# The order of a mixer's steps: from a written table to a rule of turns

## The reference

```python
h = rmsnorm(x, g_mix[l]) * (1.0 + sc1) + sh1
proj = h @ w_in[l]
q, k, v, u, c_gate, b_gate = jnp.split(proj, [A, 2 * A, 3 * A, 3 * A + C, 3 * A + 2 * C], axis=-1)
...
attn = moba_attention(heads(q), heads(k), heads(v), slopes)
attn = attn.transpose(0, 2, 1, 3).reshape(B, S, A)
conv = b_gate * causal_dwconv(c_gate * u, conv_w[l], conv_b[l])
mixed = jnp.concatenate([rmsnorm(attn, g_attn_out[l]), rmsnorm(conv, g_conv_out[l])], axis=-1)
x = x + gt1 * (mixed @ w_out[l])
```

## Time and profile before

| | |
|---|---|
| median of 3 runs | 1716.35 us |
| the profiled execution's own time | 1716.84 us |
| its span, first to last instruction | 1715.0 us |
| TensorE busy | 1676.2 us (98%) |
| VectorE, ScalarE, GpSimd busy | 1293.7 us, 929.3 us, 407.1 us |
| mean granted TensorE clock | 0.99 of full speed |
| this mixer's stretch | 1382 to 1514 us |

### The profile page before, as it was taken

One profiled execution on the slowest core, in us unless ns is written; L12 is line 12 of the kernel. 1 busy time (PEld: TensorE's weight loads), 2 busy tenths in 40 slices (PEclk: granted clock), 3 DMA queues, 4 the chain that ended last, 5 costly groups with the idle time before them and its releaser, 6 DMA issues.

```text
span 1715.0 us, 32702 instructions
## 1 busy us (share of the span) xinstructions
PE 1676.2 (98%) x13812; PEld 1523.4 (89%) x13812; DVE 1293.7 (75%) x2141; ACT 929.3 (54%) x1666; POOL 407.1 (24%) x316
## 2 busy tenths in 40 slices
PE   7999999999999999999999999999999999979997
PEld 6888998889898888888898888999888899979987
DVE  5887767866858877788776786686888776889974
ACT  5775435433546764577444543355675456466652
POOL 2763000000214661167200000021575100211110
PEclk9999999999999999999999999999999999989999
DMA  7675532211156655566562321125665553345442
GB/s 263 218 298 185 210 122 99 100 51 52 69 185 259 253 199 196 211 251 233 186 216 97 111 87 51 52 81 191 234 257 191 190 186 133 114 148 186 168 154 107
DMA packets 45057, 282.67 MB, mean 165 GB/s; under 512 B 6128, under 2 KB 6768, under 8 KB 18544
## 3 DMA queue, kind: packets, MB, share of 16 engines
q1 hardware_dynamic: 44912, 280.60, 45.3%
HBM read 279.53 MB, written 1.05 MB: 164 GB/s over the span
## 4 chain that ended last, share of the span: by engine, by line
PE 90%; DVE 6%; ACT 2%; issue 1%; DMA 1%; POOL 0%; SPq 0%; DVEq 0%; ACTq 0%
PE banks L457 28%; PE banks L458 14%; PE banks L992 11%; PE banks L449 7%; PE banks L450 7%; PE banks L451 7%; PE banks L1599 4%; DVE WL L420 2%; ACT WH L415 1%; PE banks L1868 1%; PE banks L496 1%; PE banks L1878 1%; DMA ring<-wst 1%; PE banks L664 0%; DVE XN L2502 0%
## 5 line engine op out<-in xcount | busy, mean ns | idle before, releaser
L420 DVE TENSOR_TENSOR WL<-ring,WH 128x2048 fp32r<-128x2048 f32 (+1 forms) x219 | 459.8, 2111 | 110.5 <-ACT WH L415 110.4
L457 PE MATMUL banks<-XNP,WH 128*128 128x512 f32 x1408 | 499.3, 399 | 10.8 <-DVE XNP L542 8.6
L415 ACT ACTIVATE WH<-ring 128x2048 fp32r<-128x2048 f32 (+1 forms) x223 | 380.8, 1716 | 55.8 <-PE banks L451 46.2
L458 PE MATMUL banks<-XNP,WL 128*128 128x256 f32 x1408 | 393.4, 279 | 0.0
L457 PEld LDWEIGHTS banks<-XNP,WH 128*128 128x128 f32 x1408 | 266.4, 189 | 73.0 <-DVE XNP L542 9.5
L890 POOL TENSOR_TENSOR HP<-G,HP 128x256 fp32r<-128x256 f32 x110 | 210.1, 1911 | 310.3 <-ACT HP L702 310.3
L457 PE MATMUL banks<-HP,WH 128*128 128x512 f32 x770 | 267.5, 392 | 0.8 <-POOL HP L890 0.7
L458 PEld LDWEIGHTS banks<-XNP,WL 128*128 128x128 f32 x1408 | 267.1, 190 | 0.0
L458 PE MATMUL banks<-HP,WL 128*128 128x256 f32 x770 | 215.2, 280 | 0.0
L992 PE MATMUL banks<-XN,ring 128*128 128x256 f32 x832 | 192.5, 381 | 0.0
L457 PEld LDWEIGHTS banks<-HP,WH 128*128 128x128 f32 x770 | 144.6, 188 | 33.3 <-POOL HP L890 1.4
(11 more groups left out here) (496 smaller groups left out, 3255.3 us busy)
## 6 DMA issues: line engine op xcount, KB each, us to landing
ring<-wst SPq DMA_DIRECT2D x205, 1024.0 KB, 4.9
ring<-wst SPq DMA_DIRECT2D x80, 704.0 KB, 4.0
LP<-lp SPq DMA_DIRECT2D x1, 1872.0 KB, 7.4
LP<-lp SPq DMA_DIRECT2D x4, 448.0 KB, 5.6
ring<-wst SPq DMA_DIRECT2D x2, 512.0 KB, 5.5
X<-xin SPq DMA_DIRECT2D x2, 512.0 KB, 6.3
out<-X SPq DMA_DIRECT2D x4, 256.0 KB, 2.2
C<-cst SPq DMA_DIRECT2D x1, 193.0 KB, 5.0
```

The lines of the kernel that those rows point to most:

```text
L415: e.do.activation(WH[:, slot[q], 0:n], ring[:, i % NSLOT, 0:n], ACT.Copy).then_inc(*w_act.up("high", q))
L420: e.do.tensor_tensor(WL[:, slot[q], 0:n], ring[:, i % NSLOT, 0:n], WH[:, slot[q], 0:n].bitcast(F32), ALU.subtract).then_inc(*w_dve.up("low ...
L457: e.do.matmul(b[:, :], WH[:, s, cols], x.rearrange("p s t -> p (s t)"), start=first, stop=False)
L458: return e.do.matmul(b[:, 0:T], WL[:, s, cols], x[:, 0, :], start=False, stop=last)
```

## The change

The table is replaced by a function that builds the list. `in_turns` goes round a fixed cycle of names; each time it comes to a name whose strand has steps left and whose need is met (counts of steps done by other strands), it appends that name. `second_order_of` gives the cycle and the needs.

```diff
+def in_turns(steps, turns, needs, allowed=None):
+    done, out = dict.fromkeys(steps, 0), []
+    while any(done[s] < steps[s] for s in steps):
+        before = len(out)
+        for turn in turns:
+            s = turn.split()[0]
+            if s != turn and not allowed(turn, done):
+                continue
+            if done[s] < steps[s] and needs(s, done[s], done):
+                out.append(s)
+                done[s] += 1
...
+    turns = ["proj", "conv", "att0", "att1", "proj", "att2", "att3", "norm0", "first", "norm1"]
...
+        if s == "conv":
+            return done["proj"] >= min(2 * in2_at(5, k) + 4, steps["proj"])
+        if s in attends:
+            j = attends.index(s)
+            return done["proj"] >= {0: 2 * in2_at(1, j) + 4, 4: 2 * in2_at(2, j) + 6}.get(k, 0)
+        if s == "norm1" and k == 0:
+            return done["conv"] == steps["conv"] and done["first"] >= 6
+        if s == "norm1" and k == 2:
+            return done["first"] == steps["first"]
+        if s == "norm0" and k == 0:
+            return all(done[n] == steps[n] for n in attends)
+        if s == "first":
+            return done["proj"] == steps["proj"] and done["norm0"] == steps["norm0"]
...
-SECOND_TURNS = """
-proj*10 att1 att0 proj*3 att1 proj*3 att0 proj*2 att1 proj*2 att0 att1 att3 proj*6 att0 att3*2 att2 att1 att0
...
-            orders[l] = turns(MIXER_TURNS) if l < DEPTH else turns(SECOND_TURNS)
+            orders[l] = turns(MIXER_TURNS) if l < DEPTH else second_order_of(steps)
```

More of the change, by code:

```diff
@@ L188, in wait_ge, with second_order_of, needs @@
             self.do.wait_ge(sem, n)
+def in_turns(steps, turns, needs, allowed=None):
[9 more added lines that the diff above has]
+                done[s] += 1
+        assert len(out) > before, done
+    return out
+def second_order_of(steps):
+    attends = [f"att{j}" for j in range(4)]
+    turns = ["proj", "conv", "att0", "att1", "proj", "att2", "att3", "norm0", "first", "norm1"]
+    def needs(s, k, done):
+        if s == "conv":
[11 more added lines that the diff above has]
+            return done["proj"] == steps["proj"] and done["norm0"] == steps["norm0"]
+        return True
+    return in_turns(steps, turns, needs)
 MIXER_TURNS = """
@@ L204 @@
 fin ssd fin*2 ahead*4 fin ahead*2
-"""
-SECOND_TURNS = """
-proj*10 att1 att0 proj*3 att1 proj*3 att0 proj*2 att1 proj*2 att0 att1 att3 proj*6 att0 att3*2 att2 att1 att0
-att1 att0 att1 proj att2 proj att3 proj att1 proj att0 proj*2 att0*2 proj*2 att2*2 att0 att3 att2 att3 att2
-proj att3 att1 proj att2 proj*3 att2 att3 proj att3 proj*2 att2 att3 conv*2 att1 att2 proj norm0 proj norm0
-proj*2 norm0 proj*2 first conv first*3 conv first*2 norm1 first*2 norm1*2
 """
```

## The result

The changed kernel has a median of 1725.14 us over 5 timed runs (1723.57 to 1726.16), the kernel before 1716.35 us (1714.70 to 1716.84) beside it. The ratio is 1.0052, with a 95% interval of 1.0040 to 1.0063: slower. The forecast was 1721.2 us with a range of 1718.0 to 1724.4. The sign and the places of the three waits were right; the size was too small by 3.9 us, and the range ended 0.7 us too low.

What follows compares the result with a forecast made beforehand. TensorE was taken to bound the projection stretch. Waits of 0.93 + 1.66 + 1.54 = 4.13 us plus 0.72 for scattering gave +4.85, so 1721.7 us for the profiled execution and 1721.2 for the median, range 1718.0 to 1724.4.

Steps and rivals of the forecast that it cites:

- the three waits: New TensorE waits at tile 6 and at pairs 2 and 3's first products with v: 4.13 us together.
- TensorE sets the pace of the stretch: From second to last projection tile TensorE is busy 80.96 of 81.20 us, so each new wait counts in full.
- tile 6: Projection tile needing tile 4's bias, its evacuation queued behind scores on VectorE: wait 1.17 us instead of 0.24, net +0.93.
- the products with v: Pairs 2 and 3's first products, close behind ScalarE's copy of v: waits of 1.66 and 1.54 us.
- Scattering: Eight more returns of TensorE to the projection at 0.09 us each: +0.72 us, bounds 0 and 0.8.
- The end of the list: Behind the last projection tile, conv 3 and norm1 1 earlier: cost 0, hidden by VectorE's 2.19 us idle.
- Rival A: The waits come and TensorE's clock falls to half in the stretch too: 1722.9 to 1724.6 us; chance 15%.
- Rival B: Waits in the stretch shrink to little as VectorE and ScalarE have free time: +0.5 to +3 us; chance 17%.
- Rival C: Faster: shifted clock fall at norm1 frees up to 2.2 us of VectorE's wait for the norm's row, 1713.9 us; chance 6%.

Runs made afterwards that it cites:

- e1: The changed kernel again with no edit, for a second profile: 1724.11 us, ratio 1.0047 to the kernel before.
- e3: Changed kernel with pairs 0 and 1's second-head scores one projection step earlier and pair 3's first product with v one later: 1720.42 us, ratio 1.0019.
- e4: Changed kernel with the edits of e3, and the first scores of pairs 0 and 1 together again as before: 1720.87 us, ratio 1.0023.
- e7: Kernel before with the transposes of pair 1's second head moved into the group of pair 0's, one break fewer: 1716.28 us.
- e8: Kernel before with only the changed list's end (conv 3 two steps earlier, norm1 1 ahead of first 7): 1715.48 us.
- e12: The changed kernel's order with the same added filler matmuls as e11: 1722.16 us, ratio 1.0022.
- e11: Kernel before with the filler matmuls of e9 and e10, plus two ahead of the mixer's first tile: 1714.15 us, ratio 0.9976.
- e6: Kernel before with six attention pieces moved one to six projection steps from their groups, four breaks more: 1717.54 us.
- e9: Kernel before with three filler matmuls in TensorE's wait ahead of norm1's sums: 1717.84 us, ratio 0.9996.
- e5: The kernel before again, its list written out, order unchanged: 1717.67 us, ratio 1.0007.
- e10: Kernel before with 9, 3 and 4 filler matmuls in three waits of the norm after the output projection: 1716.37 us, ratio 0.9994.

## Why the prediction was right and wrong

- **TensorE sets the pace of the stretch, so each wait counts in full: shown.** Taking out 2.82 us of waits shortened the stretch by 2.65, with one return more (e1 to e3), taking out 3.64 by 3.77 (e1 to e4, 97.22 to 93.45).
- **Three waits, at these places, from the chain behind the scores: right.** 1.01, 1.45 and 1.38 us; predicted 1.17, 1.66 and 1.54. Less the old 0.24 that is 3.60 instead of 4.13. Each is 0.16 to 0.21 short, and the timeline says why. Counted from the end of the scores, as the prediction did, tile 6 started after 2.66 us (1401.89 + 0.59 = 1402.48 to 1405.14) where I had 2.67, and the products with v after 3.87 and 3.88 where I had 3.89. So the chain over VectorE and ScalarE was right to 0.02 us. TensorE's idle time began later than I had it: at 1.65, 2.42 and 2.50 us instead of 1.50, 2.23 and 2.35. At tile 6 this is the way of counting named under e7: 0.16 us of the wait isn't idle in the profile. The 0.24 of before leaves out the same 0.16, so the wait adds 1.01 - 0.24 = 0.77, and my 0.93 came from setting a wait counted one way against a wait counted the other. At the two products only 0.07 us is hidden so, since an unhindered product starts 0.21 us behind the last projection matmul; they add 1.52 and 1.45. The rest of what I was off by there is the price of breaks again: the way out and the longer single product filled a part of the wait. Together the waits are worth 3.74 us, where 4.13 was forecast.
- **Scattering: the step that failed.** The prediction has 8 x 0.09 = 0.72 us with an upper bound of 0.8. It measured 2.72 us in e4, 0.34 per return, and 6.62 - 3.74 = 2.88 in the changed kernel. I had priced the return to the projection and neither the way out to scores or a product (0.09, ten more times in the changed kernel) nor the longer single pieces, and I set the bound at the value itself, though rows that showed a group and a single piece side by side were at hand (0.85 single, 1.51 for two). With 2.88 for 0.72 and 3.74 for 4.13 the sum is 6.62, that of the stretch, 1.8 us more than forecast.
- **The range.** This alone would not have left it: 1716.35 + 6.62 is 1723.0. The other 2.2 us between that and the measured median are not in the stretch, and the prediction had no term for them. See the last point.
- **The end of the list: right at 0 where the clock falls** (e8, and the -0.02 us of the table). The prediction hung this on VectorE's 2.19 us of idle time, and it was right to: without a fall that time is gone, and the end costs 0.33 us (e3, e12).
- **Rival A, the clock falling in the stretch: wrong.** It stayed at 1.00 through all three waits, 1.45 us the longest. Its prices were too high as well: at norm1 6.83 us low costs 2.8 us in its own part and 1.3 to the end of the kernel, not 3.4. Wide matmuls follow the three waits. That the same idle time ahead of one-column matmuls is followed by a fall fits, but e3 and e7 show that even there it isn't always. That the width decides is not shown.
- **Rival B: wrong.** No wait shrank by more than 0.21 us.
- **Rival C's mechanism exists.** VectorE's wait for the norm's row is 1.70 us in the changed kernel, no such wait is left in e3, where the clock doesn't fall, and up to 2.8 us come back at norm1, of which 1.3 are left at the end of the kernel. Here it gave nothing in the two profiled executions, and it was too small to turn the sign.

VectorE's timeline of the changed kernel, which answers to the earlier trace rows:

```profile
1496.71 0.42 DVE L2534 TENSOR_TENSOR RV<-banks,RV 128x256 f32<-128x256 f32 x1
1497.17 0.48 DVE L2537 SCALAR_TENSOR_TENSOR XN<-RV,MOD,XN 128x256 f32<-128x256 f32 x1
1499.36 0.42 DVE L2534 TENSOR_TENSOR RV<-banks,RV 128x256 f32<-128x256 f32 x1 [1.70 <-ACT RV L2454]
```

- **The last 1 to 2 us: they go with the clock, and why is open.** The stretch explains 6.6 of the 8.8 us between the medians (and 6.5 of 8.0 between e11 and e12). Each timed execution comes with its mean granted clock, and set beside those with the same clock the changed kernel is no further off than its stretch: at 0.989 it takes 1725.35 us on average (7 executions) and the kernel before 1718.46 (20), 6.9 apart; at 0.990 it is 1723.83 (8) and 1717.32 (31), 6.5 apart, all timed executions of both kernels taken together. With the fillers, at 0.995, e12 takes 1720.70 (2) and e11 1714.17 (8), 6.5 apart. Averages over all executions are 7.5 us apart, and what that has over the stretch goes with the changed kernel's lower clock (0.9894 on average, before 0.9899); the 8.8 of the first medians, of five executions each, is above all of these. Where those falls are, only the profiled executions tell. In them the clock also fell ahead of the mixer, at about 261 or 959 us, in all six kernels with the new order or most of it (the changed kernel, e1 to e4, e12), and in four of the eight others, with before's order or nearly (e6, e7, e9, e11, and not before, e5, e8, e10). First e1 and then before, a stretch in the first model where both run the same instructions:

```profile
256.00:270.00 14.00, 13.03 (x49) 8.64 (x48) 9.32 (x23) 9.46 (x25) 0.00 (x0) 0.76 0.13 30
```
```profile
256.00:270.00 14.00, 13.03 (x63) 9.47 (x62) 10.09 (x26) 9.36 (x26) 0.00 (x0) 1.00 0.21 75
```

  With such a fall at 261 us the mixer's second tile starts at 1394.3 to 1395.5 us, with one at 959 us at 1392.7 to 1393.2, with neither at 1391.1 to 1392.4. That would make up the rest if such falls are commoner with the new order. Six of six against four of eight is too few to say so, and nothing in the profile shows how a later order could act on them. It stays open. Nor do medians resolve everything: e3 and e4 have stretches 1.1 us apart and nearly equal medians (1720.42, 1720.87).

## What to carry to other kernels

Ahead of regrouping an in-order queue, price an excursion by all its edges: leaving, each piece alone and not as a share of a group, and the return. Here that was 0.34 us a time on average, 8 more times, nearly as dear as the waits, and an excursion of transposes alone only about 0.08. Then count, for every consumer right behind a producer, what stands ahead of the producer on its own engine: scores one step ahead of a copy cost 1.4 us twice, and moving them two steps away gave it back. When clock falls elsewhere come and go with the execution, compare the stretch between two fixed matmuls, or executions with the same mean clock, and not the totals.

## What was unexpected of the hardware

- The same code with the same wait of 1.35 us ahead of it met the 1.2 GHz level for 6.83, 3.41 or 0 us from one execution to the next. The Trainium skill (TensorE: Matmul & The Clock Gate, What's actually happening) ties the clock to activity and says that the same kernel shows another number of slow matmuls from run to run. The second the rows bear out (6.83, 3.41, 0). As to the first, that the clock stayed up at norm1 in all three profiled executions with three filler matmuls there, 1.46 us together (e9, e11 and e12), agrees. But it stayed up in three of the eleven without them too (e3, e7 and e10), so activity at this place alone doesn't decide it.
- A stretch at the low clock cost less than half of its length: 2.8 us for 6.83 at norm1 (1.3 to the end of the kernel), and 0.7 for 10.24 at the next norm, where TensorE waits much of the time.
- Going from the projection's matmuls straight to scores or to a product with v costs 0.09 us on average, coming back 0.10; going to a pair's transposes costs nothing, coming back from them 0.08. Whether the shape does that (64 rows or columns instead of 128) was not tried.
